# Projections of a hybrid decoder block as plain float32 products of 64 columns in pairs, with 8 MB of expert weights loaded ahead

## What is computed

```python
h = rms_norm(x, mix_norm_w)
proj = h @ w_in                     # 1024 x 7744: z, xbc, dt, q, six k/v of 256, gates
y_ssm = mamba2_mixer(z, xbc, dt_raw, ...)        # convolution, chunked scan, gated norm
y_nsa = nsa_mixer(q, k_c, v_c, k_s, v_s, k_w, v_w, nsa_gate, ...)  # compressed, selected, window
merged = g_ssm * (y_ssm @ w_branch_ssm) + g_nsa * (y_nsa @ w_branch_nsa)
x = x + merged @ w_out
h = rms_norm(x, ffn_norm_w)
for e in range(32):                 # each token chooses 4 of 32 experts
    a = clamped_swiglu(h @ w_gate_up[e] + b_gate_up[e])      # 1024 x 2048
    out = out + combine[:, e:e+1] * (a @ w_down[e] + b_down[e])  # 1024 x 1024
return rms_norm(x + out, final_norm_w)
```

## Time and profile before

| what | value |
|---|---|
| runs | 1250.74 us median of 3 (1250.71 to 1251.38) |
| profiled execution, by the clock that times the runs | 1250.38 us |
| its span, first to last instruction | 1248.7 us |
| TensorE busy | 1189.7 us, 95% |
| VectorE busy | 437.2 us, 35% |
| ScalarE busy | 287.7 us, 23% |
| GpSimd busy | 110.4 us, 9% |
| read from device memory | 451.88 MB |

### The profile page before, as it was taken

How to read it: one execution, slowest core, us unless ns; L and a number is a source line. 1 busy time by engine, 2 the same in 40 slices (tenths; PEclk the granted TensorE clock), 3 DMA queues, 4 the chain that set the end, 5 groups by cost and what they waited for, 6 DMA issues and landing times.

```text
span 1248.7 us, 16280 instructions
## 1 busy us (share of the span) xinstructions
PE 1189.7 (95%) x6644; PEld 623.0 (50%) x6644; DVE 437.2 (35%) x869; ACT 287.7 (23%) x521; POOL 110.4 (9%) x97
## 2 busy tenths in 40 slices
PE   8999999999999999999898989899999999999996
PEld 8999988788743434433342424333343434243432
DVE  7776667767331231312122221212221212122212
ACT  6574457653410101101010100010110101010112
POOL 2302213345400000000000000000000000000000
PEclk9999999999999999999999999999999999999999
DMA  8747434339999999999999999999999999999996
GB/s 272 209 145 233 161 110 135 102 103 393 398 421 400 435 415 433 432 429 430 434 430 434 430 434 429 431 434 431 434 428 434 431 431 432 430 436 428 424 428 248
DMA packets 61565, 453.58 MB, mean 363 GB/s; under 512 B 9160, under 2 KB 33872, under 8 KB 45392
## 3 DMA queue, kind: packets, MB, share of 16 engines
q1 hardware_dynamic: 61216, 452.75, 88.3%
q10 hardware_dynamic: 304, 0.20, 0.1%
HBM read 451.88 MB, written 1.05 MB: 363 GB/s over the span
## 4 chain that ended last, share of the span: by engine, by line
PE 63%; DMA 29%; DVE 3%; ACT 3%; issue 1%; POOL 0%; SPq 0%; DVEq 0%; ACTq 0%
PE psum L1311 23%; DMA ring<-in_w_gate_up_dram 14%; DMA slot<-in_w_gate_up_dram 12%; PE psum L1323 11%; PE psum L940 9%; PE psum L1281 5%; PE psum L906 4%; PE psum L1349 3%; PE psum L842 3%; DMA ring<-in_w_down_dram 3%; PE psum L943 2%; ACT WH L1482 1%; ACT XDT L1661 1%; PE psum L1191 1%; DVE XDT L2139 1%
## 5 line engine op out<-in xcount | busy, mean ns | idle before, releaser
L1311 PE MATMUL psum<-ring,ZS 128*64 128x512 f32 x1512 | 344.7, 600 | 13.9 <-DMA ring<-in_w_gate_up_dram 13.5
L1311 PEld LDWEIGHTS psum<-ring,ZS 128*64 128x64 f32 x1512 | 105.0, 137 | 217.2 <-issue 194.3
L2285 DVE TENSOR_TENSOR X<-X,psum 128x1024 f32<-128x1024 f32 x62 | 72.9, 1217 | 370.8 <-PE psum L1349 370.7
L1323 PE MATMUL psum<-ring,HT 128*64 128x512 f32 x736 | 173.3, 625 | 22.6 <-DMA ring<-in_w_down_dram 22.6
L2267 DVE TENSOR_SCALAR ZS<-psum 128x512 f32<-128x512 f32 x32 | 22.1, 691 | 300.9 <-PE psum L1311 300.9
L1311 PE MATMUL psum<-slot,ZS 128*64 128x512 f32 x512 | 116.5, 597 | 7.7 <-DMA slot<-in_w_gate_up_dram 7.7
L1323 PEld LDWEIGHTS psum<-ring,HT 128*64 128x64 f32 x736 | 59.1, 143 | 129.5 <-issue 128.6
L1799 DVE TENSOR_TENSOR WL<-ring,WH 128x2048 fp32r<-128x2048 f32 (+1 forms) x42 | 95.9, 2285 | 37.9 <-ACT WH L1482 37.6
L1711 ACT ACTIVATE HT<-psum 128x512 f32<-128x512 f32 x31 | 18.5, 597 | 318.2 <-PE psum L842 318.2
L1482 ACT ACTIVATE WH<-ring 128x2048 fp32r<-128x2048 f32 (+1 forms) x42 | 78.9, 1878 | 9.8 <-PE psum L906 6.8
L1311 PEld LDWEIGHTS psum<-slot,ZS 128*64 128x64 f32 x512 | 34.4, 137 | 74.2 <-issue 58.8
(11 more groups left out here) (380 smaller groups left out, 1215.8 us busy)
## 6 DMA issues: line engine op xcount, KB each, us to landing
ring<-in_w_gate_up_dram SPq DMA_DIRECT2D x38, 4096.0 KB, 29.4
ring<-in_w_down_dram SPq DMA_DIRECT2D x18, 4096.0 KB, 30.8
slot<-in_w_gate_up_dram SPq DMA_DIRECT2D x12, 4096.0 KB, 28.9
ring<-in_w_gate_up_dram SPq DMA_DIRECT2D x15, 2048.0 KB, 13.4
ring<-in_w_in_dram SPq DMA_DIRECT2D x29, 1024.0 KB, 7.2
slot<-in_w_down_dram SPq DMA_DIRECT2D x7, 4096.0 KB, 30.8
ring<-in_w_down_dram SPq DMA_DIRECT2D x9, 2048.0 KB, 14.7
slot<-in_w_gate_up_dram SPq DMA_DIRECT2D x8, 2048.0 KB, 13.8
```

The costliest lines, as they stand in the source:

```text
L1311: ins = mm(psum[64 * (c % 2):64 * (c % 2) + 64, c // 2, :], XTS[:, k, s], every_other_run(row, c), start=False, stop=(k == KT - 1))
L1323: ins = mm(psum[64 * h:64 * h + 64, 2, :], lhs, w[:, at:at + 512], start=(k == 0), stop=(k == 7))
L2285: v.tensor_tensor(xo, xo, psum[:, 3 + 2 * t:5 + 2 * t, :], ALU.add).then_inc(o_read, 1)
```

## The change

- The projections take the weights as they land in the ring, and the activations, as plain float32. Each product of 128 stationary columns becomes two of 64, which write the two halves of the PSUM partitions. A narrow unit has 32 such products (before: 48), a wide one 16 (before: 24), the small unit 8 of 64 columns (before: 24).
- The splits of weights and activations on ScalarE and VectorE are gone, with their buffers, and so are the tokens `W`, `L` and `YL`. `HTH`, `OTH` and `YSH` are now float32, and ScalarE's copy alone makes them.
- TensorE waits for a unit's load (`ring_full`) instead of for its split. SP loads unit u when unit u - 4 is done on TensorE.
- The eight pieces of the ring that held parts are free from the start. 8 MB of expert weights go there early: place 1 (second half of expert 0's gate and up weights) at mg 4 and mg 6, place 3 (second unit of the loop) at bs 0 and bs 2. What is left at the end of the mixers comes in another order.
- The four filler products ahead of the last router product (line 1233) are float32 of 64 columns as well.

The diff, cut to its core:

```diff
-        HTL = at_place("HTL", [P, KT, SEQ], slot_at[STREAM])
-        OTL = at_place("OTL", [P, KT, SEQ], slot_at[STREAM + 1])
-        WH = [at_place(f"WH{i}", [P, SLOT], slot_at[STREAM + 2 + 2 * i]) for i in range(SPLITS)]
-        WL = [at_place(f"WL{i}", [P, SLOT], slot_at[STREAM + 3 + 2 * i]) for i in range(SPLITS)]
-        MTL = at_place("MTL", [P, KT, SEQ], qt_at)
-        HTH = at_place("HTH", [P, KT, SEQ], ht_at)
+        HTH = at_place("HTH", [P, KT, SEQ], ht_at, F32)
...
+            ahead = {("mg", 4): lambda: load_half(gate_up_rows(0, 1), 1, 0),
+                     ("mg", 6): lambda: load_half(gate_up_rows(0, 1), 1, 1),
+                     ("bs", 0): lambda: early_load(1, 0), ("bs", 2): lambda: early_load(1, 1)}
...
                 if u >= STREAM:
-                    if u - STREAM in SPLIT_UNITS:
-                        low_ready(sp, SPLIT_UNITS.index(u - STREAM))
-                    else:
-                        sp.wait_ge(unit_done, u - STREAM + 1)
+                    sp.wait_ge(unit_done, u - STREAM + 1)
                 full = ring_full[u % STREAM]
+                if (kind, m) in ahead:
+                    ahead[(kind, m)]()
...
             sp.wait_ge(pool_set, 3)
             sp.dma_start(once_row, unit_rows(3, 0, 4)[:, 2048:2 * 2048]).then_inc(once_full, 16)
-            sp.wait_ge(unit_done, at_unit[("bn", 3)] + 1)
-            load_half(gate_up_rows(0, 1), 1, 0)
-            low_ready(sp, len(SPLIT_UNITS) - 3)
-            low_ready(sp, len(SPLIT_UNITS) - 2)
-            early_load(0, 1)
             sp.wait_ge(mt_full, 4)
             once_quarter(0)
-            sp.wait_ge(unit_done, at_unit[("wo", 1)] + 1)
-            early_load(1, 0)
-            low_ready(sp, len(SPLIT_UNITS) - 4)
-            low_ready(sp, len(SPLIT_UNITS) - 1)
-            early_load(0, 0)
             sp.wait_ge(unit_done, at_unit[("wo", 2)] + 1)
-            early_load(1, 1)
+            early_load(0, 1)
             sp.wait_ge(unit_done, NU)
-            load_half(gate_up_rows(0, 1), 1, 1)
+            early_load(0, 0)
             sp.wait_ge(pool_set, 4)
             sp.wait_ge(h2_ready, 4)
             once_quarter(1)
...
-                for n, (w, src) in enumerate([(wh, high), (wh, low), (wl, high)]):
-                    if w is wl and t == 0:
-                        low_ready(pe, i)
-                    if n == 1 and kind == "wo":
-                        pe.wait_ge(mt_low, 2 * h + t + 1)
-                    for k in range(4):
-                        ins = mm(bank(b, 512), src[:, 4 * h + k, P * t:P * t + P], w[:, k, :],
-                                 start=(h == 0 and n == 0 and k == 0), stop=(h == 1 and n == 2 and k == 3))
+                src = {"bs": YSH, "bn": OTH}.get(kind, HTH)
+                w = slot_view(u, 4, 512)
+                if t == 0:
+                    pe.wait_ge(ring_full[u % STREAM], full_at[u])
+                for k in range(4):
+                    for c in (0, 64):
+                        ins = mm(bank(b, 512)[c:c + 64], src[:, 4 * h + k, P * t + c:P * t + c + 64], w[:, k, :],
+                                 start=(h == 0 and k == 0), stop=(h == 1 and k == 3))
...
+                thirds = (0, 3, 6, KT)
+                for k in range(thirds[n0], thirds[n1]):
+                    for c in (0, 64):
+                        at = slice(P * half + c, P * half + c + 64)
                         if feature_major:
-                            ins = mm(bank(b, 2, SEQ)[:, half], w[:, k, rows], src[:, k, :],
-                                     start=(n == 0 and k == 0), stop=(n == 2 and k == KT - 1))
+                            ins = mm(bank(b, 2, SEQ)[c:c + 64, half], w[:, k, at], HTH[:, k, :],
+                                     start=(k == 0), stop=(k == KT - 1))
...
-                mm(bank(7, SEQ), HTH[:, 0, 0:P], HTH[:, 1, :], start=True, stop=True)
+                mm(bank(7, SEQ)[0:64], HTH[:, 0, 0:64], HTH[:, 1, :], start=True, stop=True)
```

More of the change, by code:

```diff
@@ L165, in token_order @@
     out += [("H0", last), ("XX", 2), ("H1", last), ("RM", 2), ("P0", last), ("X3", 0), ("P1", last)]
[L168 to L178, removed]
-        else:
[L180 to L187, removed]
+    return out
 TOKENS = token_order()
@@ L924, in half_unit @@
                 feature_major = kind in ("xbc", "kc", "vc", "ks", "kw", "q", "z")
-                high, low = (HTH, MTL) if kind == "wo" else (HTH, HTL)
-                rows = slice(P * half, P * half + P)
                 nco = 256
-                i = SPLIT_UNITS.index(u)
-                wh, wl = part(WH[i % SPLITS], 0, KT, nco), part(WL[i % SPLITS], 0, KT, nco)
+                w = slot_view(u, KT, nco)
                 if half == 0 and n0 == 0:
-                    pe.wait_ge(wh_ready, i + 2)
-                passes = [(wh, high), (wh, low), (wl, high)]
-                for n in range(n0, n1):
-                    w, src = passes[n]
-                    if w is wl and half == 0:
-                        low_ready(pe, i)
-                    for k in range(KT):
+                    pe.wait_ge(ring_full[u % STREAM], full_at[u])
+                thirds = (0, 3, 6, KT)
+                for k in range(thirds[n0], thirds[n1]):
+                    for c in (0, 64):
+                        at = slice(P * half + c, P * half + c + 64)
                         if feature_major:
-                            ins = mm(bank(b, 2, SEQ)[:, half], w[:, k, rows], src[:, k, :],
-                                     start=(n == 0 and k == 0), stop=(n == 2 and k == KT - 1))
-                        else:
-                            ins = mm(bank(b, 2, nco)[:, half], src[:, k, rows], w[:, k, :],
-                                     start=(n == 0 and k == 0), stop=(n == 2 and k == KT - 1))
+                            ins = mm(bank(b, 2, SEQ)[c:c + 64, half], w[:, k, at], HTH[:, k, :],
+                                     start=(k == 0), stop=(k == KT - 1))
+                        else:
+                            ins = mm(bank(b, 2, nco)[c:c + 64, half], HTH[:, k, at], w[:, k, :],
+                                     start=(k == 0), stop=(k == KT - 1))
                 if half == 1 and n1 == 3:
@@ L957, in small_unit @@
             def small_unit(u):
-                b, i = bank_of[u], SPLIT_UNITS.index(u)
+                b = bank_of[u]
                 pe.wait_ge(proj_free[b], freed[u])
-                wh, wl = part(WH[i % SPLITS], 0, KT, 64), part(WL[i % SPLITS], 0, KT, 64)
-                pe.wait_ge(wh_ready, i + 2)
-                for n, (w, src) in enumerate([(wh, HTH), (wh, HTL), (wl, HTH)]):
-                    if w is wl:
-                        low_ready(pe, i)
-                    for k in range(KT):
-                        ins = mm(psum[0:64, b, 0:SEQ], w[:, k, :], src[:, k, :],
-                                 start=(n == 0 and k == 0), stop=(n == 2 and k == KT - 1))
+                w = slot_view(u, KT, 64)
+                pe.wait_ge(ring_full[u % STREAM], full_at[u])
+                for k in range(KT):
+                    ins = mm(psum[0:64, b, 0:SEQ], w[:, k, :], HTH[:, k, :], start=(k == 0), stop=(k == KT - 1))
                 ins.then_inc(unit_done, 1)
@@ L1825, in _ @@
             dve.sem_inc(par_ready, 1)
-            split(1)
             def last_added(t):
```

157 lines of the change are left out of this document (41 added, 116 removed).

## The result

The changed kernel takes **1309.82 us** (median of 4 runs, 1309.39 to 1310.19) where the kernel before took 1250.72 us beside it (median of 4, 1250.19 to 1251.38). The ratio is 1.0472, its 95% interval 1.0454 to 1.049: 59.1 us slower. The forecast was 1308 us, its range 1299 to 1322.

A forecast was written before the change was run, and what follows sets the result against it. TensorE was taken to bound the mixers, the expert weight stream the rest, so the end follows the experts' begin. Terms put that 60.1 us later, less 3.0: +57.1, forecast 1308 us, range 1299 to 1322.

The forecast's parts named there:

- Narrow units, +27.8: Narrow projections on TensorE: a unit takes 6.92 us, 1.16 more than before; 24 units add 27.8 us.
- Wide units, +25.6: Wide projections on TensorE: a unit takes 6.88 us instead of 5.46; 18 units add 25.6 us.
- The small unit, +0.6: Small projection unit, whose 64 columns have no partner: 3.5 us against 2.9 before, adding 0.6 us.
- Fillers and router, +0.9: Four float32 filler products near the router take 1.7 us instead of 0.5, so the last router product comes 0.9 us later.
- Switching, +7.3: TensorE alternating between projections and full 128-column products in 52 blocks: 0.14 us each, adding 7.3 us.
- whole drains: Rival, chance 0.07: each switch waits a product's whole duration, 0.34 us a block instead of 0.14; up to 1322 us.
- VectorE and ScalarE, nothing but -2.1 of stalls: Dropped conversions and subtractions were hidden behind TensorE and worth nothing, except 2.1 us of TensorE stalls inside attention rounds.
- Late loads, nothing: Projection loads wait longer for a ring slot but still go out early enough, so they cost nothing.
- the backlog, -3.0: Expert weight stream as the experts begin: 8 MB loaded early gains only the 3.0 us it was behind.
- early bytes in full: Rival, chance 0.06: the stream also limits when the experts begin, so early loads take off 19.5 us, giving 1291 us.
- no overlap: Rival, chance 0.03: the two column halves do not overlap, units cost 13.8 us, 290 us more, 1600 us.
- cheap pairs: Rival, chance 0.02: a pair of 64-column products takes one record's stream, 91 us off TensorE, between 1168 and 1209 us.

The follow-up runs named there:

- full columns: The changed kernel with plain float32 projection products of 128 columns instead of 64 in pairs, in all units: 1302.22 us.
- the one with four halves last: The changed kernel with all four early expert-weight halves (8.4 MB) issued only after the last projection unit: 1323.24 us.
- the one with two halves last: The changed kernel with two of the four early expert-weight halves (4.2 MB) issued only after the last projection unit: 1313.67 us.
- the first experiment: The changed kernel with the four early expert-weight halves (8.4 MB) loaded at the end of the mixers again, as in the kernel before: 1309.09 us.
- kernel before with the delay: The kernel before with 100 instead of 4 filler products just ahead of the last router product: 1261.72 us.

## Why the prediction was right, and where it was not

- *Narrow units, +27.8.* A unit of 6.91 us for 6.92 forecast, from rows of 64 column products at two other sizes. Seven in a row took 48.35 us instead of 40.32: +1.15 each, 27.5 for 24.
- *Wide units, +25.6.* 3.43 us for eight pairs of records, where 3.44 was forecast.
- *The small unit, +0.6.* From its first product to the next unit 2.73 us before, about 3.3 after.
- *Fillers and router, +0.9.* +1.03 in the timeline; the run with one filler confirms the cause.
- *Switching, +7.3.* Undoing the pairs brought the experts forward by 7.3 us, and the wide half of the blocks alone by 3.2. That compares pairs with full columns and not with the split products of the kernel before. That these two start their blocks alike is shown only by the sum: with full columns the experts begin 51.2 us later than before, and the other terms as measured (27.5 + 25.6 + 0.5 + 1.0 - 3.0) make 51.6. The rows gave 0.11 to 0.24 us a block and 0.14 was picked between them; that the total came out to the tenth is luck. Here a lone narrow unit with its transposes loses 0.30, a round of the attention (from half a wide unit to the next) 0.10: 255.23 - 249.61 = 5.62 us in pairs, 5.52 with full columns. This spread was not forecast. The rival of whole drains (0.34 a block) falls.
- *VectorE and ScalarE, nothing but -2.1 of stalls.* TensorE's idle time from the second unit to the experts fell from 2.32 us (320.15 us, busy 317.83) to 0.22 (377.50, busy 377.28). That is the 2.1. The run without VectorE's weight splits moved the experts by 3.0, of which 1.8 were idle time and 1.2 time in which TensorE reads as busy; I take those for products that started late behind other work, which no row shows. The term was short by some 0.9 us, if this carries over to the change, for which no run was made.
- *Late loads, nothing.* No projection waited for the ring in the changed kernel.
- *The experts' begin.* 60.1 us later in the sum, 58.5 measured. With the figures above the terms are 27.5 + 25.6 + 0.5 + 1.0 + 7.3 - 3.0 = 58.9.
- **The step that failed is the backlog, -3.0.** It came to nothing: the distance from the experts' begin to the end was 911.9 us before and 913.4 after, and 911.4 to 913.4 in all kernels but the two with loads behind the last unit. The prediction said that the stream is the limit from the moment the experts begin, and is ahead or behind by its backlog. The rows say otherwise. The backlog of the kernel before only filled the time in which a queue that has run empty brings nothing: 20 us behind the experts' begin the change is ahead by 0.2 MB, 0.5 us, and not by 3. And for 200 us TensorE works without a gap; the stream is not at its full rate there, and 2.6 us of lag are caught up without a product being late. Only behind that stretch does the stream bound the kernel, and by 100 us it is in the same place in every kernel that had at most 2.1 MB issued late (344.2 or 344.3 MB to come). The two errors, -1.6 on TensorE's side and +3.0 to +4.5 on the stream's, left the total 1.8 us low; that they had opposite signs is luck.

The mechanism in one line: end of the span = begin of the experts + 912 us + what is issued behind the last projection beyond 6 us of stream. It gives the end of all twelve kernels, before and after among them, within 1.5 us. The 912 and the 6 are themselves taken from these kernels, the 6 from the one with four halves last; the one with two halves last was forecast with it (1313.4 us, measured 1313.67).

Of the rivals, "early bytes in full" falls by the first experiment, "whole drains" by the full columns, and "no overlap" and "cheap pairs" by the unit of 6.91 us. No run came out as a version that is faster than the kernel before and still computes everything: the best with plain float32 was full columns, 1302.2 us.

## What to carry to other kernels

Before costing freed work on an engine, ask whether the stage waits for that engine: 91 us off VectorE were worth 3.5 us here, while 11.8 and 12.0 us more on TensorE just ahead of the experts cost 11.0 and 11.3. For a stream that follows a compute stage, find out how far it may lag before the first product is late; loads moved earlier inside that slack bring nothing, and backlog is not time gained. Pairs of half tiles in place of full ones streamed no faster and cost a little at every change of form; where tiles are half empty no run here tells what pairs are worth.

## What the runs showed of the hardware

- Two float32 products of 64 columns in the two column halves together took as long as one of 128 columns: 6.91 against 6.92 us for a unit of 256 moving columns.
- A plain float32 unit took 1.20 times a three-pass float32r one (6.91 against 5.76 us). The wide form pays more, 6.87 against 5.46, 1.26 times, because the float32r products of 512 columns took 0.227 us each, and two of 256 took 0.24.
- A change between the paired form and the full one cost 0.10 us a round in the attention and 0.30 us around a lone narrow unit; the transposes behind such a unit took 0.58 us instead of 0.44 with full columns.
- When the queue had run empty, the full rate came about 2 us behind the issue: issue at 397.31 us, rates of 113 and 133 GB/s up to 399.2, 420 from there. In the kernel before with the delay, whose DMA engines stood still, the issue was at 350.58 us and the first weight packets started 0.95 us later.
- GpSimd's busy time fell from 110.4 to 84.8 us when VectorE's weight splits were left out, with the same 97 instructions (84.9 in the change). Its five elementwise operations on 1024 float32 columns of `XDT` took 3.08 us each in the kernel before and 1.89 without the splits; those on 512 columns of `E` took 1.30 in both. Why, no run shows. In the chain that ended last GpSimd has 0% or does not appear.
